# The last head group's operands and the samples' state products in an RWKV-7 and sparse attention step

## The reference

```
xs = p_rw + (prev - p_rw) * mu_shift                       # token shift of the projection's rows
r, k, v, wd, ad, gd = split_cols(xs, RW_SPLITS)
w = -softplus(-(w0 + tanh(wd) @ w_decay_up)) - 0.5         # rate of decay
a = sigmoid(a0 + ad @ w_a_up)                              # in-context rate
kk = heads(k * k_k);  kk = kk / max(sqrt(sum(kk * kk)), 1e-12)
k_h = heads(k) * (1 + (a - 1) * k_a);  decay = exp(-exp(w));  b_h = kk * a
S = S * decay - (S @ kk) b_h^T + v k_h^T;  y = S @ r       # a scan over positions, one matrix state per head
bonus = sum(r_h * k_h * r_k) * v_h
out = (groupnorm(y) + bonus) * g
```

## Time and profile before

| | |
|---|---|
| median of 3 runs | 1136.01 us (1131.51 to 1138.15) |
| profiled execution | 1138.8 us, span of its trace 1136.9 us |
| mean granted TensorE clock | 0.986 |
| busy share of the span | TensorE 96%, VectorE 62%, ScalarE 35%, GpSimd 56% |
| projection with the preparation of the last group | to about 245.8 us |
| RWKV's first (samples') tile up to its `pe_from_v` | 245.8 to 266.7 us |

### The profile page before, as it was taken

How to read it: one execution, slowest core, us unless ns; L and a number is a source line. 1 busy time by engine, 2 the same in 40 slices (tenths; PEclk the granted TensorE clock), 3 DMA queues, 4 the chain that set the end, 5 groups by cost and what they waited for, 6 DMA issues and landing times.

```text
span 1136.9 us, 23859 instructions
## 1 busy us (share of the span) xinstructions
PE 1088.8 (96%) x9685; PEld 1023.6 (90%) x9693; DVE 703.8 (62%) x1219; ACT 395.2 (35%) x748; POOL 631.1 (56%) x687
## 2 busy tenths in 40 slices
PE   9999999979888999999999999999999999999996
PEld 7978989868787889888899999999999999999995
DVE  7972766774566488675244334686368547735786
ACT  6343334433233433333331112343134224413453
POOL 7832556652322055623346655678568757866783
PEclk9999999989999999999999999999999999999998
DMA  7443532220100331222242223222223132213122
GB/s 250 109 81 61 95 102 66 65 82 3 40 3 4 109 93 57 59 82 74 66 140 74 75 74 107 75 70 75 93 76 91 57 97 88 66 51 111 51 75 93
DMA packets 48337, 89.29 MB, mean 79 GB/s; under 512 B 6728, under 2 KB 11216, under 8 KB 48048
## 3 DMA queue, kind: packets, MB, share of 16 engines
q1 hardware_dynamic: 43568, 77.88, 22.2%
q10 hardware_dynamic: 4672, 10.04, 4.4%
HBM read 80.06 MB, written 7.83 MB: 77 GB/s over the span
## 4 chain that ended last, share of the span: by engine, by line
PE 68%; DVE 22%; issue 4%; ACT 3%; POOL 2%; DMA 1%; SPq 0%; ACTq 0%; DVEq 0%; POOLq 0%
PE acc L792 17%; PE acc L793 11%; PE wk L1423 8%; PE acc L1423 7%; PE wk L792 6%; PE wk L793 4%; PE wk L950 2%; DVE hid_lo L2433 1%; PE acc L1000 1%; DVE invs L2223 1%; PE acc L1025 1%; PE wk L1305 1%; DVE xT L2028 1%; PE acc L1278 1%; DVE score L2091 1%
## 5 line engine op out<-in xcount | busy, mean ns | idle before, releaser
L681 POOL TENSOR_TENSOR w_lo<-w_raw,w_hi 128x512 fp32r<-128x512 f32 x178 | 244.0, 1371 | 14.8
L678 POOL TENSOR_TENSOR w_hi<-w_raw,ones_w 128x32 fp32r<-128x32 f32 x178 | 59.4, 334 | 317.1 <-PE acc L793 259.3
L792 PE MATMUL acc<-h_hi,w_hi 128*128 128x384 f32 x424 | 150.7, 356 | 3.9 <-POOL w_lo L681 1.7
L792 PE MATMUL acc<-h_lo,w_hi 128*128 128x384 f32 x424 | 143.9, 339 | 0.0
L792 PE MATMUL acc<-h_hi,w_lo 128*128 128x384 f32 x424 | 143.7, 339 | 0.0
L679 POOL TENSOR_SCALAR w_hi<-w_raw 128x480 fp32r<-128x480 f32 x178 | 120.7, 678 | 0.1
L793 PE MATMUL acc<-h_hi,w_hi 128*128 128x256 f32 x424 | 118.8, 280 | 0.0
L793 PE MATMUL acc<-h_lo,w_hi 128*128 128x256 f32 x424 | 118.8, 280 | 0.0
L793 PE MATMUL acc<-h_hi,w_lo 128*128 128x256 f32 x424 | 118.7, 280 | 0.0
L792 PEld LDWEIGHTS acc<-h_hi,w_hi 128*128 128x128 f32 x424 | 80.1, 189 | 12.2 <-issue 6.5
L756 POOL TENSOR_TENSOR p_lo<-w_sum,p_hi 128x512 fp32r<-128x512 f32 x44 | 64.9, 1479 | 29.6 <-ACT p_hi L1937 29.6
(11 more groups left out here) (455 smaller groups left out, 3132.3 us busy)
## 6 DMA issues: line engine op xcount, KB each, us to landing
w_raw<-w SPq DMA_DIRECT2D x178, 256.0 KB, 2.6
w_block<-w SPq DMA_DIRECT2D x64, 256.0 KB, 2.9
line_scratch<-line ACTq DMA_DIRECT2D x8, 384.0 KB
xT<-xT SPq DMA_DIRECT2D x4, 640.0 KB, 6.7
x<-xT ACTq DMA_DIRECT2D x1, 2560.0 KB, 9.1
bias_p<-line_scratch SPq DMA_DIRECT2D x8, 256.0 KB, 4.3
kc<-k_cache SPq DMA_DIRECT2D x8, 256.0 KB, 2.6
vc<-v_cache SPq DMA_DIRECT2D x8, 256.0 KB, 2.6
```

What stands on the lines that cost most here:

```text
L678: nc.gpsimd.tensor_tensor(hi[:, s, 0:LEAD], w_raw[:, r, 0:LEAD], ones_w[:], ALU.mult).then_inc(w_high, 1)
L681: nc.gpsimd.tensor_tensor(lo[:, s, :], w_raw[:, r, :], hi[:, s, :].bitcast(F32), ALU.subtract).then_inc(w_split, 1)
L792: mm(out[:, 0:CUT], w_, x_[:, k0 + b, 0:CUT], start=go, stop=end)
```

## The change

The rates `sgz` and `aa` get two buffers, used in turn, and ScalarE's rates wait for the group two back. `kh` moves from `prep_rates` into `prep_operands`, with the bonus product of the group before between its two instructions. For the last group, the key squares stand between the two `gemm`s of tile 22 instead of behind them, ScalarE's root stands ahead of that tile's copies and stores, and the bonus operand is written behind `bt` and `kt`. The load of `s_all` stands four `w` units earlier on SP and has another place in memory; the samples' state products stand behind the first pairs and the first turn instead of behind the third level's parts. In the first two RWKV tiles VectorE writes all four masks before it starts an inverse.

```
-    sgz = at("sgz", W0 + 19.25, [P, T])
+    sgz = [at(f"sgz{n}", W0 + (0, 19.25)[n], [P, T]) for n in range(2)]
-    aa = at("aa", W0 + 24.25, [P, T])
+    aa = [at(f"aa{n}", W0 + (2.5, 24.25)[n], [P, T]) for n in range(2)]
-    s_all = at("s_all", W0 + 31.25, [P, NB, 4, HD])
+    s_all = at("s_all", W0, [P, NB, 4, HD])
...
-            load_units(PAIR, U_GATE + 4)
-            sp.wait_ge(bonus_set, 4)
-            sp.wait_ge(prep_set, 4)
+            load_units(PAIR, U_GATE)
+            sp.wait_ge(codes_mm, 4)
+            sp.wait_ge(prep_set, 3)
             sp.dma_start(s_all[:]...).then_inc(s_landed, 16)
+            for u in range(U_GATE, U_GATE + 4):
+                load_at(u)
...
                 gemm(2 * n, ...)
+                if phase(n) == (4, 0):
+                    key_squares(3)
                 gemm(2 * n + 1, ...)
...
-                if step == 0 and 1 <= j <= 4:
+                if step == 0 and 1 <= j <= 3:
                     key_squares(j - 1)
...
             pe_turn(0, 0)
+            pe_samples_state(1)
+            pe.wait_ge(turn_set, 1)
+            pe_samples_state(0)
             for level in range(merges(0)):
                 for p in range(2):
                     pe_part(0, level, p)
                 if level == 0:
-                    pe.wait_ge(turn_set, 1)
+                    pe.wait_ge(start_set, 2)
                     pe_turn(0, 1)
                 if level == 1:
                     pe_turn(0, 2)
-                if level == 2:
-                    pe.wait_ge(turn_set, 2)
-                    pe_samples_state(0)
-                    pe.wait_ge(turn_set, 3)
-                    pe_samples_state(1)
...
+            def key_root(j):
+                act.wait_ge(ksq_max, j + 1)
+                do(A(kk[:], nrm[:], ACT.Abs_reciprocal_sqrt), ksq_root)
...
+                if phase(n) == (4, 0):
+                    key_root(3)
                 act.wait_ge(w_used, 2 * n + 2)
...
-                    if j >= 1:
-                        act.wait_ge(prep_set, j)
+                    z, a_ = sgz[j % 2], aa[j % 2]
+                    if j >= 2:
+                        act.wait_ge(prep_set, j - 1)
                     act.wait_ge(codes_mm, j + 1)
...
                     act.wait_ge(*freed(RW_AT[3 * j + 3]))
+                    if j:
+                        act.wait_ge(rkb_set, j)
                     do(A(e1[:], kxs[:, j % 2, :], ACT.Square, scale=v("k_k", j)), ksq_set)
...
             act_turned(0, 0)
+            for n in (1, 0):
+                act.wait_ge(start_mm, 2 - n)
+                do(A(from_state[:]..., ACT.Copy), start_set)
             act_part(0, 0)
...
+            for n in range(2):
+                for p in range(2):
+                    dve_pairs(0, n, p)
             for p in range(2):
-                dve_pairs(0, 0, p)
                 dve_first(0, p)
-            for p in range(2):
-                dve_pairs(0, 1, p)
```

More of the change, by code:

```diff
@@ L396, in build @@
     e_masks = at("e_masks", W0 + 46, [P, E_COLS])
-    br = [at(f"br{q}", W0 + (18.25, 0)[q], [P, NH, 2, HD]) for q in range(2)]
-    invs = [at(f"invs{q}", W0 + (22.25, 4)[q], [P, 2, 2, 4, HD]) for q in range(2)]
+    br = [at(f"br{q}", W0 + (18.25, 31.25)[q], [P, NH, 2, HD]) for q in range(2)]
+    invs = [at(f"invs{q}", W0 + (22.25, 35.25)[q], [P, 2, 2, 4, HD]) for q in range(2)]
     part = at("part", W0 + 8, [P, NH, HD])
@@ L1158, in _ @@
             pe.wait_ge(fv_mm, 1)
-            pe.wait_ge(start_set, 2)
             for a in range(2):
@@ L1634, in _ @@
                 if step == 1 and 0 <= j <= 3:
-                    if j >= 1:
-                        act.wait_ge(prep_set, j)
+                    z, a_ = sgz[j % 2], aa[j % 2]
+                    if j >= 2:
+                        act.wait_ge(prep_set, j - 1)
                     act.wait_ge(codes_mm, j + 1)
-                    do(A(sgz[:], wk_lo[:, 0:T], ACT.Tanh, bias=half_b[:, j:j + 1], scale=0.5))
-                    do(A(aa[:], wk_hi[:, 0:T], ACT.Tanh, bias=half_b[:, 4 + j:5 + j], scale=0.5))
+                    do(A(z[:], wk_lo[:, 0:T], ACT.Tanh, bias=half_b[:, j:j + 1], scale=0.5))
+                    do(A(a_[:], wk_hi[:, 0:T], ACT.Tanh, bias=half_b[:, 4 + j:5 + j], scale=0.5))
                     do.settle()
-                    do(A(sgz[:], sgz[:], ACT.Identity, bias=eps_c[:, 2:3], scale=0.5), rates_set)
-                    do(A(aa[:], aa[:], ACT.Identity, bias=eps_c[:, 2:3], scale=0.5), rates_set)
+                    do(A(z[:], z[:], ACT.Identity, bias=eps_c[:, 2:3], scale=0.5), rates_set)
+                    do(A(a_[:], a_[:], ACT.Identity, bias=eps_c[:, 2:3], scale=0.5), rates_set)
                 if step == 2 and 0 <= j <= 3:
                     act.wait_ge(*freed(RW_AT[3 * j + 3]))
+                    if j:
+                        act.wait_ge(rkb_set, j)
                     do(A(e1[:], kxs[:, j % 2, :], ACT.Square, scale=v("k_k", j)), ksq_set)
                     act.wait_ge(cum_set, j + 1)
-                    do(A(e0[:], sgz[:], ACT.Exp, scale=-DECAY_C), exps_set)
+                    do(A(e0[:], sgz[j % 2][:], ACT.Exp, scale=-DECAY_C), exps_set)
                 if step == 0 and 1 <= j <= 4:
                     j -= 1
-                    act.wait_ge(ksq_max, j + 1)
-                    do(A(kk[:], nrm[:], ACT.Abs_reciprocal_sqrt), ksq_root)
+                    if j < 3:
+                        key_root(j)
                     act.wait_ge(ksq_mm, j + 1)
@@ L1704, in _ @@
             act_turned(0, 0)
+            for n in (1, 0):
+                act.wait_ge(start_mm, 2 - n)
+                do(A(from_state[:].rearrange("p j a c -> p (j a) c")[:, :, HD * n:HD * n + HD],
+                     wk[:, 2 + n, :].rearrange("p (g c) -> p g c", g=8), ACT.Copy), start_set)
             act_part(0, 0)
@@ L1709, in _ @@
             act_part(0, 2)
[L1710 to L1713, removed]
             for e in range(2):
@@ L2117, in prep_rates @@
             def prep_rates(j):
+                z = sgz[j % 2]
                 dve.wait_ge(rates_set, 2 * j + 2)
-                do(V.tensor_tensor_scan(cum[:], reset[:], sgz[:], 0.0, ALU.mult, ALU.add))
-                do(V.tensor_scalar(kh[:], aa[:], v("k_a", j), oka[:, j:j + 1], ALU.mult, ALU.add))
+                do(V.tensor_tensor_scan(cum[:], reset[:], z[:], 0.0, ALU.mult, ALU.add))
                 do.settle()
-                do(V.tensor_tensor(sgz[:], cum[:], sgz[:], ALU.subtract), cum_set)
-                do(V.tensor_tensor(kh[:], kh[:], kxs[:, j % 2, :], ALU.mult))
+                do(V.tensor_tensor(z[:], cum[:], z[:], ALU.subtract), cum_set)
             def prep_operands(j, following):
+                a_ = aa[j % 2]
                 dve.wait_ge(ksq_mm, j + 1)
                 do(V.tensor_scalar(nrm[:], wk_lo[:, 0:T], 1e-24, None, ALU.max), ksq_max)
+                do(V.tensor_scalar(kh[:], a_[:], v("k_a", j), oka[:, j:j + 1], ALU.mult, ALU.add))
+                if j:
+                    prep_bonus(j - 1)
+                do.settle()
+                do(V.tensor_tensor(kh[:], kh[:], kxs[:, j % 2, :], ALU.mult))
                 dve.wait_ge(ksq_root, j + 1)
@@ L2141, in prep_operands @@
                 do(V.scalar_tensor_tensor(ar[:, j, :, 0, :], tiles(kk[:]), -1.0, tiles(e0[:]), ALU.mult, ALU.mult), a_set)
-                do(V.tensor_tensor(aa[:], aa[:], kk[:], ALU.mult))
+                do(V.tensor_tensor(a_[:], a_[:], kk[:], ALU.mult))
                 if following in RW_AT:
@@ L2148, in prep_operands @@
                 do.settle()
-                do(V.scalar_tensor_tensor(r, r, v("r_k", j), kh[:], ALU.mult, ALU.mult), rkb_set)
+                if j < 3:
+                    do(V.scalar_tensor_tensor(r, r, v("r_k", j), kh[:], ALU.mult, ALU.mult), rkb_set)
                 dve.wait_ge(exps_set, 3 * j + 3)
-                do(V.tensor_tensor(bt[:, j, :], aa[:], e0[:], ALU.mult))
+                do(V.tensor_tensor(bt[:, j, :], a_[:], e0[:], ALU.mult))
                 do(V.tensor_tensor(kt[:, j, :], kh[:], e0[:], ALU.mult), prep_set)
+                if j == 3:
+                    do(V.scalar_tensor_tensor(r, r, v("r_k", j), kh[:], ALU.mult, ALU.mult), rkb_set)
             def prep_bonus(j):
@@ L2286, in _ @@
                 dve_pairs(1, 0, p)
-                dve_first(1, p)
             dve.wait_ge(fv_mm, 1)
@@ L2290, in _ @@
                 dve_pairs(1, 1, p)
+            for p in range(2):
+                dve_first(1, p)
             dve_y_centre(0)
```

2 lines of the change are left out of this document (removed).

## The result

The changed kernel takes 1132.2 us (median of 20 executions, 1120.9 to 1135.1) against 1139.6 for the kernel before (20 executions, 1131.2 to 1144.7): a ratio of 0.993, with an interval of 0.990 to 0.995. It is 7.4 us faster where 13.3 were forecast, and 9.5 us above the forecast time.

A forecast was written before the change was run, and what follows sets the result against it. A VectorE-then-TensorE chain, with TensorE's waits and low-clock matmuls behind them, was taken as the bound. 8.6 + 5.2 - 0.5 = 13.3 us off 1138.8 gives 1125.5 profiled, 1122.7 for the median; range 1116.5 to 1130.

The forecast's parts named there:

- Gain 8.6: Projection up to the first RWKV tile's pairs: pairs start at 237.2 instead of 245.8 us, bounds 10 to 5.
- the 1.7 us wait with its low clock: TensorE's wait for the `vt` shift goes, 1.7 us, and the 0.57 clock directly behind it, another 1.7.
- the late root: Last group: the 2.8 us wait for ScalarE's root goes, since it no longer stands behind copies and three DMA issues.
- So it moves whole: Everything after the changed stretch waits for it, so the full 13.3 us come off the execution time.
- a smaller gain: Rival: low clock only moves, VectorE's last products at upper bounds, second inverse start blocked; gain 8.7, 1127.3 us, chance 0.21.
- Samples' products behind the first pairs, masks first: First RWKV tile, from pairs to `pe_from_v`: 15.7 us instead of 20.9, gain 5.2 (6 to 4).
- Masks first, second tile: Second RWKV tile: inverse starts now stand behind the masks of `kr`; cost 0.5 us (0 to 1.5).
- Key squares earlier: Tile 22, between its `gemm`s: Square over at 212.8, 0.9 us before TensorE comes, so its wait costs nothing.
- it would cost 5 without the buffers: Tile 22: if the rate buffers did not act, TensorE's wait for the Square of `kxs` would be 5 us.
- Remaining wait for `rx`: Before the last bonus sums: bonus operand ready at 235.8, 1.3 us behind the last `gemm`, ends 0 and 3.0.
- State's load: `s_all` load on SP: landed by about 221 us, some 19 before TensorE asks, delaying four `w` loads by 0.4.
- no change in the projection: Rival: buffers do not make the Square earlier, TensorE stands 5.5 us in tile 22; 1131.3 us, chance 0.07.

The follow-up runs named there:

- the wait filled: Changed kernel, TensorE repeating the next tile's value turn five times instead of once while waiting for the state, tiles 1 to 3: 1120.1 to 1122.9 us, ratio 0.984.
- the two other pairs of profiles: Kernel before against changed kernel, start of first pairs: both run again without edit, 2.1 us; both with four added repeats of the turn, 2.8 us.
- the repeats alone: Kernel before with four added repeats of TensorE's turn of the next tile's values: 1129.7 us against 1141.6, ratio 0.992.
- the state first and two repeats: Changed kernel, state update ahead of `kr` masks in tiles 1 to 4, turn three times, second tile's old inverse-start order: 1118.0 us, ratio 0.985.

## Why the prediction was wrong

**The step that failed** is "Gain 8.6", the gain up to the first pairs. As a reading of that one execution it was too small: the pairs came 12.8 us earlier, 1.5 of which lie ahead of the change (the first codes started at 119.0 instead of 120.5, behind a stretch from 80 to 90 us that has 0.83 in the first of the two profiles and 1.00 in the second). As the gain of the change it was at least twice too large: 4.2 by the traces with the wait filled, and 2.1 to 2.8 by the two other pairs of profiles. Three terms of it, the 1.7 us wait with its low clock, the late root and the rest of the wait for `rx`, were taken from the earlier trace rows as the kernel's, but a second execution has 0.6 us for `vt`, 0.8 for the root (2.8 in the earlier trace rows) and 0.65 for `rx`.

**"So it moves whole"** holds between executions that are alike, which the two profiles weren't. The forecast named the risk ("if some other stretch falls to the lower level in turn") and priced it at 1.7, here and in the rival "a smaller gain"; it costs 11 to 12 in four tiles, which the rows of its one execution don't show. And it isn't caused by the change: of the executions whose clock is known, 15 of 24 of the changed kernel have it, and 37 of 53 before. With such a spread a median of three can lie far off: 1136.0 was 3.6 below that of twenty. The clocks of those three aren't known.

**Samples' products behind the first pairs, masks first**: right. `pe_from_v` at T + 15.2 (forecast 15.7; T, the start of the pairs, is 233.0 in the changed profile), gain 4.8 (5.2). The first update began at T + 8.4 (8.3), the second inverse was ready at T + 7.1 (7.2). One of the two starts was held up, 1.36 us, and the other took 0.43, as assumed. The Trainium skill ("SBUF — State Buffer", Who interferes with whom) would have allowed both to be held up; the trace has one.

**Masks first, second tile**: cost 0.5, measured 0.6. **Key squares earlier**: costed at nothing, right; the Square ended at 209.8 and TensorE came at 211.5. That it would cost 5 without the buffers was right too (4.9). **Root**: no wait, right. **Remaining wait for `rx`**: 1.3 forecast, none measured; the last product on VectorE ended at 230.6 instead of 235.8, and TensorE came at 231.7 instead of 234.5. **State's load**: issued at 212.07 and never waited for, right.

**The sum** by the measured terms is 4.2 + 4.8 - 0.6 = 8.4 (6.3 with the smallest front, 2.1), between the 7.4 with the wait filled and the 9 to 10 between executions at the same clock. From 1139.6 it gives 1131.2; measured 1132.2. Of the 9.5 us that the forecast missed, 3.6 are the median of three it started from, 4.4 the front, 0.5 the two other terms, and 1.0 is left. The size of the gain is that of the rival "a smaller gain" (8.7), but not by its reasons. The time lies next to the rival "no change in the projection" (1131.3) by chance: its sign, a wait for `e`, isn't in the profile of the change. It is chance too that the changed kernel's upper group (1121.4) lies close to the forecast's 1122.7.

**What stays open**: why the same 2.7 us wait is followed by the lower level in all tiles of one execution and in none of another. The Trainium skill ("TensorE: Matmul & The Clock Gate", What's actually happening) says, of the slow matmuls at a kernel's start, that the gate's watch runs freely instead of starting with the kernel, and that the outcome differs from run to run. The two profiles of one program agree in that they differ, though in the middle of a kernel (0.57 and 1.00 behind 2.75 and 2.74 us); no run here shows what the chip looked at.

Open as well is how often the front of the kernel before is as late as in the forecast's profile, the only one of four with the old front that shows it, and whether the front's gain is nearer to 2 or to 4 us.

## What to carry to other kernels

Before a wait and the slow matmuls behind it are booked as a gain, look at a second profile and at the clock of every execution: what only one execution shows is not the kernel's. Where the times fall into two groups by the clock, compare each group with its like, and sum the change from stretches at the same level. A wait of a few microseconds that returns in every turn of a loop is worth filling with idle repeats, or shortening at its source; here the repeats alone gave the kernel before as much as the whole change (ratios of 0.992 and 0.993).

## What the hardware showed that was not expected

- The four tiles mostly fell together or not at all: in the two profiles of the changed kernel all four and none fell, in the two of the kernel before one and all four. Without the fill 52 of 77 executions of the two lie at a clock of 0.982 or less, and the groups are 11 to 12 us apart.
- The lower level also came behind waits of 0.94 and 1.08 us, in the kernel with the state first and two repeats.
- Sixteen more transposes in each of three tiles didn't move the end of the wait they stand in: from `pe_from_v` to the first product of `state` behind it, 10.04 us with them (279.88 to 289.92) and 10.04 without (281.35 to 291.39).
- The same DMA issue on ScalarE's queue took 0.48 us in eleven of the twelve profiles and 1.91 in one, where what stood behind it on the engine waited 1.2 us.
